# Latent attention: four heads scored together, as 64-row and 32-row products, instead of one head at a time with 96 rows

## The reference, cut to what matters

```python
MLA_HEADS, MLA_NOPE, MLA_ROPE, MLA_V = 16, 64, 32, 64
MLA_QK = MLA_NOPE + MLA_ROPE          # 96
scale = MLA_QK ** -0.5
key_chunk = jnp.arange(s) // CHUNK_2  # chunks of 64 positions
...
sc = jnp.einsum('bqhd,bkhd->bhqk', qi, k) * scale   # blocks of 128 queries
mask = key_chunk[None, :] <= q_chunk[:, None]
p = jax.nn.softmax(jnp.where(mask, sc, -jnp.inf), axis=-1)
o = jnp.einsum('bhqk,bkhd->bqhd', p, v)
```

## Time and profile before

| what | value |
|---|---|
| median of three runs | 2594.36 us (2594.05 to 2594.51) |
| the profiled execution | 2593.84 us |
| its span on the core | 2591.9 us |
| granted TensorE clock, mean over the span | 1.000 |
| PE busy | 99% of the span |
| last projections, 1515 to 1558 us | PE 39.81, DVE 38.52, ACT 31.48 of 43.00 us |
| attention, 1579 to 1641 us | PE 59.86, DVE 45.88, ACT 51.11 of 62.00 us |
| last product of the attention starts | 1645.67 us |

### The profile page before, as it was taken

The page is one execution under the profiler, slowest core; times in us unless marked ns, Lnnn a source line. Parts: engine busy times, 40 slices in busy tenths (PEclk is TensorE's granted clock), DMA queues, the critical chain, the costliest instruction groups (busy, mean ns, idle before and its releaser), DMA issues.

```text
span 2591.9 us, 35040 instructions
## 1 busy us (share of the span) xinstructions
PE 2566.1 (99%) x12518; PEld 2037.7 (79%) x12518; DVE 1679.5 (65%) x2404; ACT 1281.7 (49%) x2137; POOL 363.0 (14%) x270
## 2 busy tenths in 40 slices
PE   9999999999999999999999999999999999999999
PEld 7855788888786557788888776789988777899887
DVE  4476677643988895677653688597643546687633
ACT  4326534333546895443333578567533425567432
POOL 0020100000103781100000130000620002000800
PEclk9999999999999999999999999999999999999999
DMA  5330222222243442222222220132232231232222
GB/s 214 108 92 25 96 97 97 97 97 97 81 132 126 126 130 74 89 96 94 95 97 97 95 66 17 52 126 101 82 111 97 90 104 51 98 122 99 82 97 97
DMA packets 73407, 249.17 MB, mean 96 GB/s; under 512 B 8108, under 2 KB 8236, under 8 KB 72912
## 3 DMA queue, kind: packets, MB, share of 16 engines
q1 hardware_dynamic: 72208, 239.31, 27.9%
q0 software_dynamic: 944, 8.40, 0.9%
q10 hardware_dynamic: 144, 0.00, 0.0%
HBM read 242.56 MB, written 2.24 MB: 94 GB/s over the span
## 4 chain that ended last, share of the span: by engine, by line
PE 90%; DVE 5%; ACT 2%; POOL 2%; issue 1%; DMA 0%; DVEq 0%; ACTq 0%; POOLq 0%
PE bank L391 24%; PE bank L393 24%; PE bank L392 24%; PE bank L1284 2%; PE bank L1285 2%; PE bank L1286 2%; PE bank L2181 2%; POOL xT L834 1%; PE bank L1359 1%; PE bank L1390 1%; DVE mT L459 1%; PE bank L1379 1%; PE bank L3016 1%; PE bank L1629 1%; PE bank L1618 1%
## 5 line engine op out<-in xcount | busy, mean ns | idle before, releaser
L365 DVE TENSOR_TENSOR wlo<-wraw,whi 128x1024 fp32r<-128x1024 f32 x349 | 450.8, 1293 | 451.5 <-ACT whi L342 450.9
L342 ACT ACTIVATE whi<-wraw 128x1024 fp32r<-128x1024 f32 x357 | 375.8, 1055 | 502.9 <-DMA wraw<-in_w 502.6
L391 PE MATMUL bank<-hnhi,whi 128*128 128x512 f32 (+1 forms) x1528 | 597.2, 391 | 2.4 <-DVE arena L2675 1.6
L392 PE MATMUL bank<-hnlo,whi 128*128 128x512 f32 (+1 forms) x1528 | 585.2, 383 | 0.0
L393 PE MATMUL bank<-hnhi,wlo 128*128 128x512 f32 x1392 | 542.7, 390 | 0.0
L391 PE MATMUL bank<-ahi,whi 128*128 128x512 f32 x1184 | 463.9, 392 | 1.1 <-DVE alo L654 0.4
L392 PE MATMUL bank<-alo,whi 128*128 128x512 f32 x1184 | 461.3, 390 | 0.0
L393 PE MATMUL bank<-ahi,wlo 128*128 128x512 f32 x1184 | 461.3, 390 | 0.0
L391 PEld LDWEIGHTS bank<-hnhi,whi 128*128 128x128 f32 x1528 | 287.3, 188 | 87.4 <-issue 32.0
L392 PEld LDWEIGHTS bank<-hnlo,whi 128*128 128x128 f32 x1528 | 287.5, 188 | 57.6 <-issue 3.3
L393 PEld LDWEIGHTS bank<-hnhi,wlo 128*128 128x128 f32 x1392 | 261.4, 188 | 55.4
(11 more groups left out here) (354 smaller groups left out, 3962.3 us busy)
## 6 DMA issues: line engine op xcount, KB each, us to landing
wraw<-in_w SPq DMA_DIRECT2D x410, 512.0 KB, 3.3
arena<-cs_scratch SPq DMA_DIRECT2D x20, 512.0 KB, 6.0
over_a<-cs_scratch SPq DMA_DIRECT2D x12, 512.0 KB, 6.0
arena<-in_rpb POOLq DMA_DIRECT2D x1, 2880.0 KB, 13.8
out_dram<-xT SPq DMA_DIRECT2D x8, 256.0 KB, 2.0
arena<-in_t_step POOLq DMA_DIRECT2D x2, 897.0 KB, 4.7
mT<-arena SPq DMA_DIRECT2D x28, 64.0 KB, 2.0
arena<-in_t_ab POOLq DMA_DIRECT2D x1, 1472.0 KB, 6.4
```

What stands on the lines that cost most here:

```text
L342: act.activation(whi[:, slot * BLOCK:(slot + 1) * BLOCK], wraw[:, slot * BLOCK:(slot + 1) * BLOCK], ACT.Copy).then_inc(sem("w_hi"), 1)
L365: dve.tensor_tensor(low_home(i), wraw[:, slot * BLOCK:(slot + 1) * BLOCK], whi[:, slot * BLOCK:(slot + 1) * BLOCK], ALU.subtract).then_inc ...
L391: pe.matmul(out, wh, ah, start=start, stop=False)
L392: pe.matmul(out, wh, al, start=False, stop=False)
```

## The change

The 32 items become 16 steps of two items. The two items of a step are two pairs of heads with the same block of queries, so a step has four heads and one width; `mla_block` gives the widths 1, 2, 3, 4 and then 2, 3, 4, 1 three times over (in blocks). `pe_mla_step(s)` replaces `pe_softmax` here: four matmuls of 64 rows (both heads of a pair lie in one tile, on its lower and upper half), then four of 32 rows (all four heads lie in one tile), which add into the same four banks 0 to 3. Then come values(2s-4), turn(2s-2), values(2s-3), turn(2s-1). Scores of a step wait for the maxima of both items of the step before. Transposes have banks 6 and 7 only, and a turn beside an item wider than 256 waits until ScalarE has copied the item just before it. The ring `mla_soft` grows to four. The order of DVE within an item stays.

In the projections, ScalarE and DVE write whole tiles: one copy of a query pair, one addition for the rotary part of four heads, one 128-row key, and two 32-row pieces of the rotary key. A key's bank comes free when the first of these is done (`key_read`). The keys get four banks; items start after units 26 and 28. In the state space mixer both calls of `dve_gained` move behind step 46.

```diff
-        def dve_softmax(dve, n0, items, soft, ready, hook, part=None):
+        def dve_softmax(dve, n0, items, soft, ready, hook, part=None, ring=3):
...
-                    if n >= 3:
-                        dve.wait_ge(sem("item_transposed"), n0 + n - 2)
+                    if n >= ring:
+                        dve.wait_ge(sem("item_transposed"), n0 + n - ring + 1)
...
-                if q in (36, 38):
-                    dve_gained(dve, At(q // 2 - 18))
+                if q == 46:
+                    dve_gained(dve, At(0))
+                    dve_gained(dve, At(1))
...
         def mla_turn_banks(n):
-            return (2, 3) if n % 2 == 0 else (6, 7)
+            return (6, 7) if n % 2 == 0 else (7, 6)
...
-        UNIT_BANK = [(0, 2, 3)[u % 3] for u in range(12)] + [(5, 7)[j // 6] if kind == "v" else 5 if j == 7 else (4, 7, 3)[j % 3] for kind, j in UNITS[12:]]
+        UNIT_BANK = [(0, 2, 3)[u % 3] for u in range(12)] + [(2, 7)[j // 7] if kind == "v" else (3, 7, 4, 5)[j % 4] for kind, j in UNITS[12:]]
...
-        MLA_EARLY = {24: 0, 26: 1, 28: 2}
+        MLA_EARLY = {26: 0, 28: 1}
...
-                    pe.wait_ge(sem("head_normed"), j + 1)
+                    pe.wait_ge(sem("key_read"), j + 1)
...
-                    for e in range(2):
-                        act.activation(tile(2 * j + e, 0, R0), src[e * R0:(e + 1) * R0, :], ACT.Copy,
-                                       scale=col("qgn", 0, e * R0, (e + 1) * R0))
+                    act.activation(q_plain(j), src[:, :], ACT.Copy, scale=col("qgn"))
...
-            for e in heads:
-                k, lo, by = tile(16 + 2 * j + e, 0, R1), e * HD, mla_rq(j)
-                dve.scalar_tensor_tensor(out=k[0:R0, :], in0=src[lo:lo + HD, :], scalar=col("kgn", 0, lo, lo + HD),
-                                         in1=by[lo:lo + HD, :], op0=ALU.mult, op1=ALU.mult)
-                ins = dve.tensor_tensor(k[R0:R1, :], krope(lo, lo + MLA_ROPE), by[lo:lo + MLA_ROPE, :], ALU.mult)
-            if 1 in heads:
+            by = mla_rq(j)
+            if "plain" in parts:
+                dve.wait_ge(sem("head_rsqrt"), j + 1)
+                dve.scalar_tensor_tensor(out=k_plain(j), in0=bank[UNIT_BANK[12 + 2 * j]][:, :], scalar=col("kgn"), in1=by,
+                                         op0=ALU.mult, op1=ALU.mult).then_inc(sem("key_read"), 1)
+            if "rope" in parts:
+                for e in range(2):
+                    lo = j % 2 * MLA_ROPE + e * HD
+                    ins = dve.tensor_tensor(k_rope(j // 2, lo, lo + MLA_ROPE), krope(lo, lo + MLA_ROPE), by[lo:lo + MLA_ROPE, :],
+                                            ALU.mult)
                 ins.then_inc(sem("head_normed"), 1)
...
-                for i, h in enumerate((0, 2, 1, 3)):
-                    lo = i * MLA_ROPE
-                    ins = dve.tensor_tensor(tile(4 * g + h, R0, R1), q_rope(g)[lo:lo + MLA_ROPE, :], mla_sin()[lo:lo + MLA_ROPE, :],
-                                            ALU.add)
-                ins.then_inc(sem("q_built"), 1)
+                dve.tensor_tensor(q_turned_rope(g), q_rope(g), mla_sin(), ALU.add).then_inc(sem("q_built"), 1)
...
+            dve_mla_soft(dve, (1, 3))
+            dve_key(dve, 7, ("plain",))
             dve_mla_soft(dve, (3, 5))
-            dve_key(dve, 7, (0,))
-            dve_mla_soft(dve, (5, 6))
-            dve_key(dve, 7, (1,))
+            dve_key(dve, 7, ("rope",))
...
-            return (n + 1 * (n > 3)) % 4
+            return (n // 2 + (n > 7)) % 4
...
+        def pe_mla_step(pe, s):
+            n0 = len(NA_ITEMS)
+
+            def scores(s):
+                g, b = s // 4, mla_block(2 * s)
+                w, c = (b + 1) * P, b * P
+                if s == 0:
...
+                else:
+                    pe.wait_ge(sem("item_max"), n0 + 2 * s)
+                pe.wait_ge(sem("head_normed"), 2 * g + 2)
+                for x in range(2):
+                    for e in range(2):
+                        lo, hi = rows(e)
+                        pe.matmul(bank[2 * x + e][:, 0:w], q_plain(2 * g + x, lo, hi)[:, c:c + P],
+                                  k_plain(2 * g + x, lo, hi)[:, 0:w], start=True, stop=False)
+                for x in range(2):
+                    for e in range(2):
+                        lo = x * MLA_ROPE + e * HD
+                        pe.matmul(bank[2 * x + e][:, 0:w], q_turned_rope(g, lo, lo + MLA_ROPE)[:, c:c + P],
+                                  k_rope(g, lo, lo + MLA_ROPE)[:, 0:w], start=False, stop=True).then_inc(sem("item_scored"), 1)
+
+            def turn(n):
...
+                both = n and max(w, MLA_ITEMS[n - 1]["w"]) > SEQ // 2
+                if n >= 2 or both:
+                    pe.wait_ge(sem("item_turned"), n0 + n - 1 + both)
...
+            if s < 16:
+                scores(s)
+            for x in range(2):
+                if s >= 2:
+                    values(2 * s - 4 + x)
+                if s == 17 and x == 0:
+                    pe_row(pe, "mla_o", 1, 2, 4)
+                if 1 <= s <= 16:
+                    turn(2 * s - 2 + x)
+                if s == 16:
+                    for k, lo, hi in (((0, 0, 2),), ((0, 2, 4), (1, 0, 2)))[x]:
+                        pe_row(pe, "mla_o", k, lo, hi)
```

More of the change, by code:

```diff
@@ L2732, in mla_block @@
         def mla_block(n):
-            return (n + 1 * (n > 3)) % 4
+            return (n // 2 + (n > 7)) % 4
         def mla_item(n):
-            j, b = n // 4, mla_block(n)
+            j, b, e2 = n // 8 * 2 + n % 2, mla_block(n), n % 2 * 2
             w, heads_, m = (b + 1) * P, (2 * j, 2 * j + 1), 4 * j + b
-            apart = n > 4 and b == 0
-            score = [bank[3][:, e * P:e * P + w] if apart else bank[3 - e if n == 3 else e][:, 0:w] for e in range(2)]
-            return {"w": w, "score": score, "shared": apart, "turned_before": 1 if n == 3 else 0,
-                    "max_before": 0 if apart or n == 3 else n - 1 if n == 4 or n > 5 and mla_block(n - 1) == 0 else n, "head_before": 0,
-                    "q": [tile(h, 0, R1)[:, b * P:(b + 1) * P] for h in heads_],
-                    "k": [tile(16 + h, 0, R1)[:, 0:w] for h in heads_], "bias": [mla["mmask"][:, SEQ - w:SEQ]] * 2,
+            return {"w": w, "score": [bank[e2 + e][:, 0:w] for e in range(2)], "shared": False,
+                    "bias": [mla["mmask"][:, SEQ - w:SEQ]] * 2,
@@ L2744, in mla_item @@
                     "scale": [q_scale[:, 2 * m + e:2 * m + e + 1] for e in range(2)], "minus": q_minus[:, 2 * m:2 * m + 2],
                     "v": [[vs_mla[:, t * DM + h * HD:t * DM + (h + 1) * HD] for t in range(b + 1)] for h in heads_],
-                    "out": [bank[4 + j % 2][rows(e)[0]:rows(e)[1], b * P:(b + 1) * P] for e in range(2)], "free": mla_free(n)}
+                    "out": [bank[4 + j % 2][rows(e)[0]:rows(e)[1], b * P:(b + 1) * P] for e in range(2)]}
         MLA_ITEMS = [mla_item(n) for n in range(32)]
@@ L2750, in mla_collect @@
         def mla_collect(act, j):
[L2751 removed]
+            act.wait_ge(sem("item_valued"), len(NA_ITEMS) + j // 2 * 8 + 7 + j % 2)
             act.activation(over_hn[:, j * SEQ:(j + 1) * SEQ], bank[4 + j % 2][:, :], ACT.Copy).then_inc(sem("mla_out"), 1)
[L2754 to L2756 removed]
+        def pe_mla_step(pe, s):
[4 more added lines that the diff above has]
+                if s == 0:
@@ L2765, in first @@
+            def turn(n):
+                w = MLA_ITEMS[n]["w"]
+                if n == 0:
+                    pe.wait_ge(sem("head_rsqrt"), 8)
                 if n == 1:
-                    pe.wait_ge(sem("head_rsqrt"), 8)
-                if n == 2:
-                    pe.wait_ge(sem("head_normed"), 6)
-                if n == 3:
                     pe.wait_ge(sem("proj_read"), 8)
-            def hook(pe, n, place):
-                rows_ = {(31, "end"): ((0, 0, 2),), (32, "turn"): ((1, 0, 2),), (33, "values"): ((0, 2, 3), (1, 2, 3)),
-                         (34, "values"): ((0, 3, 4), (1, 3, 4))}
-                for k, lo, hi in rows_.get((n, place), ()):
-                    pe_row(pe, "mla_o", k, lo, hi)
@@ L2776, in pe_mla_soft @@
-            pe_softmax(pe, len(NA_ITEMS), MLA_ITEMS, mla_soft, mla_turned, mla_turn_banks, first, before, hook, 0, part)
+                both = n and max(w, MLA_ITEMS[n - 1]["w"]) > SEQ // 2
+                if n >= 2 or both:
+                    pe.wait_ge(sem("item_turned"), n0 + n - 1 + both)
+                for e in range(2):
+                    pe.wait_ge(sem("item_normed"), 2 * (n0 + n) + e + 1)
+                    out, at = turn_at(mla_turn_banks, n, e, w)
+                    for c in range(0, w, P):
+                        mm = pe.transpose(out[:, at + c:at + c + P], mla_soft(n, e)[:, c:c + P], ident)
@@ new lines, in turn, with values @@
+                mm.then_inc(sem("item_transposed"), 1)
+            def values(n):
+                it, j = MLA_ITEMS[n], n // 8 * 2 + n % 2
+                w = it["w"]
```

(15 more changed lines are left out.)

77 lines of the change are left out of this document (32 added, 45 removed).

## The result

The changed kernel took 2604.64 us (median of six, 2601.19 to 2606.14) against 2594.36 for the kernel before: 10.3 us more, ratio 1.0038, 95% interval 1.0027 to 1.0048. The forecast was 2600.2 with a range of 2593.5 to 2604.0. So the sign was right, and the time lies 0.6 us above the range.

The account below looks back on a forecast made before the run. PE, busy 99%, bounds the kernel before; after the change DVE's chain sets the attention step. +7.2 (attention) + 0 (projections, start-up) - 1.4 (state space) = +5.8 us, 2600.2 against 2594.36; range 2593.5 to 2604.0.

Parts of the forecast that it names:

- The scores on PE: Attention: 64-row and 32-row tiles run side by side, a 512-wide step takes 2.97 us; 1.3 us less PE work per cycle.
- C: Attention scores: 32-row tiles go two at a time, 0.21k more in each step, +2.5 us, 2602.7; chance 0.13.
- D: Attention scores: the switch to 32-row tiles is free, 0.2 in each of 16 steps, -3.3 us, 2596.9; chance 0.10.
- G: PE time of a step's scores, 0.40 + 0.64k for k blocks: 1.04, 1.69, 2.33, 2.97 us.
- DVE's chain: Attention: next scores wait for DVE's maxima and divisions; a cycle takes 22.3 us against 20.74, +7.2 after the start-up.
- The state space part: State space mixer: with `dve_gained` moved, two PE waits of 0.41 and 1.19 us shrink or go, -1.4 us.
- The projections: Last projections: key waits go, 3.1 us at most, given back in the start-up; sum 0; no wait for a key.
- The start-up: First attention steps: scores of steps 1 to 4 wait about 1.4, 1.6, 2.4, 1.0 us, giving back the projections' gain.
- case E: Start-up: a longer PE idle (2.4 us) brings the granted clock down for some us, 5 us more, 2605; chance 0.03.
- a dearer switch: Attention scores: change from 64-row to 32-row tiles costs up to 0.4 instead of 0.2 us; in the range's high end.
- A: Attention: the forecast itself, DVE's chain sets the step; 2600.2, own range 2596 to 2603.5; chance 0.58.
- Case B: Attention: DVE's chain hides and PE stays the bound; -5.2, -3.1 and -1.4, -9.7 us in all, 2584.7; chance 0.13.

Follow-up runs that it names:

- run 4: Changed kernel with DVE doing both maxima of a step before both divisions from step 3 on; 2612.04 us, ratio 1.0065.
- run 6: run 2 with the scores' wait split: first pair waits only for the first item's maxima, second pair for the second's; 2595.68 us, ratio 1.0003.
- run 2: Changed kernel with other key banks, so key 0 no longer shares the last query product's bank; 2600.09 us, ratio 1.0025.
- run 7: run 6 with the rotary part of key 7 moved behind item 5's maxima on DVE; 2593.88 us, ratio 0.9997.
- run 9: run 7 with PE's step order scores, first turn, both values, second turn, and three buffers for turned copies; 2591.78 us, ratio 0.9988.
- run 5: Changed kernel with unread matmuls filling PE's waits ahead of the scores, at the start and in later steps; 2602.88 us, ratio 1.0032.

## Why the prediction missed by a little, point by point

**The scores on PE: right.** 2.99 us for a 512-wide step against 2.97; the cases of serial tiles (C) and of a free switch (D) are both out. C was also priced too low: by the prediction's own rule, a step is G plus the longer side, 0.21k more in every step is 8.4 us and not 2.5. The Trainium skill, TensorE: Matmul & The Clock Gate, Part 3, has 3.07 as the measured speedup of four row tiles; here it is 3.42 / 1.07 = 3.2 with the switch counted in, and its rule would have added 2.6 us that are not there.

**DVE's chain: right, in place and size.** Third cycle, from the 256-wide scores at 1601.52 to those at 1623.92: 22.40 us against 22.3 forecast and 20.74 before. Second cycle 24.06 against 23.6. The last cycle and the end, 1623.92 to the last values at 1656.54, 32.6 us, where the kernel before had 29.6 (from 1605.66 + 10.37 to 1645.67): 3.0 more, 2.7 forecast. Together, from the start of step 4 to the last values, 79.1 us (1577.46 to 1656.54) against 71.3 before (1574.33 to 1645.67): 7.7 more, 7.2 forecast. The four steps of the third cycle take 4.49, 5.71, 7.02 and 5.18 us against 4.5, 5.7, 7.0 and 5.1. The waits by which this was to be seen are shared out otherwise, though. In that cycle the scores wait 0.69 us after the 384-wide step and 0.73 after the 512-wide one, not 1.0 and 1.3; 0.65 for a division and twice 0.37 for ScalarE's copy stand at the transposes, where the prediction had, after the start-up, only ScalarE's, once, with 0.6 to 0.7. Runs 4 and 6 show the dependence: take the division out of the chain and the scores stop waiting; split the wait and 4.4 us come back. The Trainium skill, TensorEngine Tiling (Array Packing), PSUM Bottleneck, says that tiling speeds up TensorE but not the reading of PSUM. This trace agrees: the rotary part runs 3.2 times as fast as one after the other, and PE waits 10.2 us for DVE.

**The state space part: right in kind, 1.8 to 2.0 us instead of 1.4.**

**The projections: wrong in one row.** "No wait for a key in the projections" failed. Key 0 got the bank of the last query product, and waits 1.35 us until ScalarE has squared it (L2622). The wait that I removed was for DVE; that the new list of banks brings one for ScalarE I had not followed up. Run 2 prices it at 1.5 us.

**The start-up: right in its waits, wrong in their consequence. This is the step that failed.** I had the waits with 1.4, 1.6, 2.4 and 1.0 us; they are 1.13, 1.21, 2.23 and 0.73. Their effect on the clock I put aside as case E, with a chance of 0.03, a separate 5 us, and outside the range, because "rows show only 1.00". Those rows came from a kernel whose PE never had such waits in a row, so they could not speak against it. Five of six executions have a mean granted clock below 1.000, and in the profiled one it took 3.8 us. Step 4 started at 1577.46: 3.1 after the ninth item before (1574.33), which is + 3.8 for the clock, + 1.35 for key 0, - 1.8 for the earlier entry, - 0.2 for the rest. With the 7.7 of the cycles that is 10.9 at the last values; the span grew by 11.4. Of the last half microsecond some 0.4 lies at one place in the products of `mla_o`: two starts are 0.53 and 0.34 us apart (1662.30 to 1663.17, and the same in run 2) where the kernel before has 0.23 each. No wait is listed there, so its cause stays open, but "the order of banks for `mla_o` costs nothing" is not borne out.

**The sum.** At full clock + 6.8 (2601.2) against + 5.8 forecast; then 3.4 us of clock in the median. Between the two profiled spans it is + 7.6 without the clock: 0.5 more in the cycles, 1.35 for key 0, 0.5 behind the last values, and 0.6 less in the state space part and the rest of the start-up. So the 1.0 looks better than the terms are, as the execution before that was profiled is itself 0.5 under its median. The ends of the range do not come out of the terms named for them: the low end would be 2594.1, and the high end, 2.5 for serial tiles and 3.2 for a dearer switch, 2605.9, which would have held the measured time by a reason that was not there. Two causes that I had listed as rivals of each other, A and E, both happened, as E follows from A. Case B, PE as the bound, is out: it needed the waits to vanish.

## What to carry to other kernels

Banks that are all filled at once turn the reader's whole chain into a wait, whatever the matmuls save: price the time from the last score to the last maximum, with all that the reading engine does in between, before counting columns. Splitting the wait by bank (one semaphore value for each half) added no instruction and gave back 4.4 of the 5.8 us that run 2 stood above the kernel before; when an engine's order is changed, look which of the other engine's waits the later instruction serves. If a change gives TensorE waits in a row, add the clock to the sum as a consequence and not as an unlikely case of its own. Of the two ways tried, the kernel before with its side parts (2591.7) and the changed layout with four repairs (2591.8) are both about 3 us faster than the kernel before and not to be told apart; the layout itself has not been shown to gain anything.

## What the runs showed of the hardware that I had not expected

The clock fell behind waits far shorter than I had thought dangerous: 1.13, 0.55, 0.54 and 1.21 us lie ahead of the first slow block of the changed kernel, which then ran at 1.2 GHz for some 5 us. In the profiled execution of run 7 they are shorter still, 0.50, 0.98 and 0.36 us ahead of 384-wide scores that are shown with 1.55 us, where run 9 has the same scores behind the same waits with 0.92. Equal waits did not always do it: run 2 has the same ones shifted by 1.5 us and passes at 1.000 in six of eleven executions, the changed kernel in one of six. What decides between executions of one kernel stays open; no run here tells it apart. The spread of six executions, 5 us against 0.5, is itself a sign to look for: run 5, with the waits ahead of the scores filled, has 0.7 in six. It is a weak one below 2 us, since the kernel before spread over 1.9 us in 23 later executions, all at 1.000.
